# Key heads kept once and transposed in pairs, key tiles first, in a hybrid decoder block

## The reference

```python
h = rms_norm(x, norm_mix_pre)
proj = h @ w_in
u, v_sgu, q, k, v_att, gate_a, gate_b = jnp.split(proj, offs, axis=-1)
a = chunked_spatial_gating(gelu(u), gelu(v_sgu), ...)
q = partial_rotary(q.reshape(B, S, N_Q_HEADS, HEAD_DIM), positions)
k = partial_rotary(k.reshape(B, S, N_KV_HEADS, HEAD_DIM), positions)
att = sliding_window_sink_attention(q, k, v_att, sinks)   # scores of q against k in blocks of 128
merged = sigmoid(gate_a) * (a @ w_a) + sigmoid(gate_b) * (att @ w_b)
x = x + rms_norm(merged @ w_o, norm_mix_post)
hf = rms_norm(x, norm_ff_pre)
x = x + rms_norm(square(relu(hf @ w_ff_in)) @ w_ff_out, norm_ff_post)
```

## Time and profile before

| | us |
|---|---|
| median of 3 runs | 777.48 (776.97 to 778.09) |
| profiled execution, its own time | 778.64 |
| its span | 776.9 |

### The profile page before, as it was taken

The page is one execution under the profiler, slowest core; times in us unless marked ns, Lnnn a source line. Parts: engine busy times, 40 slices in busy tenths (PEclk is TensorE's granted clock), DMA queues, the critical chain, the costliest instruction groups (busy, mean ns, idle before and its releaser), DMA issues.

```text
span 776.9 us, 9953 instructions
## 1 busy us (share of the span) xinstructions
PE 764.2 (98%) x3652; PEld 642.2 (83%) x3652; DVE 528.8 (68%) x886; ACT 364.1 (47%) x607; POOL 63.6 (8%) x114
## 2 busy tenths in 40 slices
PE   7999999999999999999999999999999999999995
PEld 6888888888888888888888998888888888888885
DVE  5723577787777235875644769846885598658897
ACT  4522656665656744232225645543543345334442
POOL 2100000122223003000001200000000000000005
PEclk9999999999999999999999999999999999999998
DMA  7343132221222522326332444036102630153005
GB/s 270 117 127 108 56 106 59 79 82 55 81 77 82 196 85 78 109 82 244 90 105 76 154 145 162 28 106 248 52 1 76 240 118 1 54 204 121 0 1 109
DMA packets 92157, 81.36 MB, mean 105 GB/s; under 512 B 2896, under 2 KB 77648, under 8 KB 92112
## 3 DMA queue, kind: packets, MB, share of 16 engines
q1 hardware_dynamic: 90864, 79.70, 31.7%
q0 software_dynamic: 576, 1.05, 1.0%
q10 hardware_dynamic: 672, 0.01, 0.0%
HBM read 77.60 MB, written 3.15 MB: 104 GB/s over the span
## 4 chain that ended last, share of the span: by engine, by line
PE 92%; DVE 4%; POOL 1%; DMA 1%; issue 1%; ACT 1%; DVEq 0%; SPq 0%; POOLq 0%
PE acc L1441 27%; PE acc L1440 27%; PE acc L1439 27%; DVE w_lo L1247 1%; PE aux L1439 1%; PE aux L1441 1%; PE aux L1440 1%; DVE sum L1270 1%; PE aux L1584 1%; DMA g_pre<-in_norm_mix_pre 1%; PE aux L1583 1%; PE aux L1593 1%; PE aux L1658 1%; PE aux L1481 1%; PE acc L1612 1%
## 5 line engine op out<-in xcount | busy, mean ns | idle before, releaser
L1439 PE MATMUL acc<-actB_hi,w_hi 128*128 128x512 f32 (+1 forms) x544 | 207.0, 381 | 0.0
L1441 PE MATMUL acc<-actB_hi,w_lo 128*128 128x512 f32 (+1 forms) x544 | 205.2, 377 | 0.0
L1440 PE MATMUL acc<-actB_lo,w_hi 128*128 128x512 f32 (+1 forms) x544 | 205.0, 377 | 0.0
L965 DVE TENSOR_TENSOR w_lo<-w_raw,w_hi 128x1024 fp32r<-128x1024 f32 x72 | 87.7, 1223 | 82.7 <-ACT w_hi L682 82.1
L1441 PEld LDWEIGHTS acc<-actB_hi,w_lo 128*128 128x128 f32 x544 | 102.3, 188 | 19.0
L1440 PEld LDWEIGHTS acc<-actB_lo,w_hi 128*128 128x128 f32 x544 | 102.5, 188 | 18.2
L1439 PEld LDWEIGHTS acc<-actB_hi,w_hi 128*128 128x128 f32 x544 | 102.4, 188 | 18.1
L682 ACT ACTIVATE w_hi<-w_raw 128x1024 fp32r<-128x1024 f32 x72 | 75.4, 1052 | 71.2 <-PE acc L1441 68.8
L1440 PE MATMUL acc<-w_lo,op_hi 128*128 128x512 f32 (+1 forms) x164 | 63.6, 388 | 0.0
L1439 PE MATMUL acc<-w_hi,op_hi 128*128 128x512 f32 (+1 forms) x164 | 63.0, 384 | 0.0
L1439 PE MATMUL acc<-w_hi,actB_hi 128*128 128x512 f32 x144 | 56.1, 390 | 0.0
(11 more groups left out here) (204 smaller groups left out, 1338.9 us busy)
## 6 DMA issues: line engine op xcount, KB each, us to landing
w_raw<-in_w_in SPq DMA_DIRECT2D x44, 512.0 KB, 3.8
w_raw<-in_w_ff_in SPq DMA_DIRECT2D x32, 512.0 KB, 4.1
down_raw<-in_w_ff_out SPq DMA_DIRECT2D x16, 1024.0 KB, 6.6
w_raw<-in_w_b SPq DMA_DIRECT2D x8, 512.0 KB, 3.6
w_raw<-in_w_a SPq DMA_DIRECT2D x8, 512.0 KB, 3.5
w_raw<-in_w_o SPq DMA_DIRECT2D x8, 512.0 KB, 3.8
x<-in_x SPq DMA_DIRECT2D x4, 512.0 KB, 7.8
x<-in_x SPq DMA_DIRECT2D x1, 2048.0 KB, 8.4
```

The lines of the kernel that those rows point to most:

```text
L965: nc.vector.tensor_tensor(w_lo[:, j], w_raw[:, j], w_hi[:, j].bitcast(F32), ALU.subtract).then_inc(lo_made, 1)
L1439: nc.tensor.matmul(o, a_hi, b_hi, start=first, stop=False)
L1440: nc.tensor.matmul(o, a_hi, b_lo, start=False, stop=False)
L1441: return nc.tensor.matmul(o, a_lo, b_hi, start=False, stop=last)
```

## The change

`qk` keeps each head of k once (20 heads in place of 24), so that one transposed tile holds two different key heads and there are two k tiles in place of four. To have each head in both halves of the partitions, ScalarE writes the high part and VectorE the low part of each of the two heads into each half: four 64x512 operations on each engine for a k tile, in place of one of 128x512. The k tiles are turned first, then the q tiles; behind the four side units come 3, 3, 2 and 2 tiles. A bank and a wait now go by a tile's place in this order, not by its number. The wait for the rotated k moves ahead of the first transpose.

```diff
-NH = NQ + 2 * NKV
+NH = NQ + NKV
...
-T_FF = T_QK + KT + NKV
+QK_TILES = KT + NKV // 2
+T_FF = T_QK + QK_TILES
...
+QK_ORDER = [KT, KT + 1] + list(range(KT))
+
+
+def tiles_turned(n):
+
+    return enumerate(QK_ORDER[(0, 3, 6, 8)[n]:(3, 6, 8, 10)[n]], (0, 3, 6, 8)[n])
...
-                        nc.scalar.activation(qk[:, t, NQ:NH].rearrange("p (g r) d -> p g r d", r=2),
-                                             kv[:, 0].unsqueeze(2).to_broadcast([P, NKV, 2, HD]), ACT.Copy)
+                        nc.scalar.activation(qk[:, t, NQ:NH], kv[:, 0], ACT.Copy)
...
-                for k in range(3 * n, 3 * n + 3):
-                    act.wait_ge(turned, T_QK + k + 1)
+                for i, k in tiles_turned(n):
+                    act.wait_ge(turned, T_QK + i + 1)
...
-                            last = nc.scalar.activation(q_pair[f][0:HD, k], aux[HD * f:HD * (f + 1), k % 4], ACT.Copy)
+                            last = nc.scalar.activation(q_pair[f][0:HD, k], aux[HD * f:HD * (f + 1), i % 4], ACT.Copy)
                     else:
-                        last = nc.scalar.activation(kT_hi[:, k - KT], aux[:, k % 4], ACT.Copy)
+                        for g, half in itertools.product(range(2), range(2)):
+                            last = nc.scalar.activation(kT_hi[HD * half:HD * (half + 1), 2 * (k - KT) + g],
+                                                        aux[HD * g:HD * (g + 1), i % 4], ACT.Copy)
...
-                        last = nc.vector.tensor_tensor(kT_lo[:, k - KT], aux[:, k % 4], kT_hi[:, k - KT].bitcast(F32),
-                                                       ALU.subtract)
+                        for g, half in itertools.product(range(2), range(2)):
+                            to = (slice(HD * half, HD * (half + 1)), 2 * (k - KT) + g)
+                            last = nc.vector.tensor_tensor(kT_lo[to], aux[HD * g:HD * (g + 1), i % 4],
+                                                           kT_hi[to].bitcast(F32), ALU.subtract)
...
-                for k in range(3 * n, 3 * n + 3):
-                    if k == 0:
-                        pe.wait_ge(rotated, 1)
-                    if k == KT:
+                for i, k in tiles_turned(n):
+                    if i == 0:
                         pe.wait_ge(rotated, 2)
-                    if k >= 4:
-                        pe.wait_ge(turned_lo, T_QK + k - 3)
+                    if i >= 4:
+                        pe.wait_ge(turned_lo, T_QK + i - 3)
                     for t in range(TT):
-                        m = nc.tensor.transpose(aux[:, k % 4, t * P:(t + 1) * P],
+                        m = nc.tensor.transpose(aux[:, i % 4, t * P:(t + 1) * P],
                                                 qk[:, t, 2 * k:2 * k + 2].rearrange("p h d -> p (h d)"), ident[:])
```

More of the change, by code:

```diff
@@ L29 @@
+import itertools
 from contextlib import ExitStack
@@ L1068, in _ @@
             for n in range(SIDE_AHEAD):
-                for k in range(3 * n, 3 * n + 3):
-                    dve.wait_ge(turned_hi, T_QK + k + 1)
+                for i, k in tiles_turned(n):
+                    dve.wait_ge(turned_hi, T_QK + i + 1)
                     if k < KT:
                         for f in range(2):
-                            last = nc.vector.tensor_tensor(q_pair[f][HD:P, k], aux[HD * f:HD * (f + 1), k % 4],
+                            last = nc.vector.tensor_tensor(q_pair[f][HD:P, k], aux[HD * f:HD * (f + 1), i % 4],
                                                            q_pair[f][0:HD, k].bitcast(F32), ALU.subtract)
                     else:
-                        last = nc.vector.tensor_tensor(kT_lo[:, k - KT], aux[:, k % 4], kT_hi[:, k - KT].bitcast(F32),
-                                                       ALU.subtract)
+                        for g, half in itertools.product(range(2), range(2)):
+                            to = (slice(HD * half, HD * (half + 1)), 2 * (k - KT) + g)
+                            last = nc.vector.tensor_tensor(kT_lo[to], aux[HD * g:HD * (g + 1), i % 4],
+                                                           kT_hi[to].bitcast(F32), ALU.subtract)
                     last.then_inc(turned_lo, 1)
```

## The result

The changed kernel takes 780.36 us (median of 6 runs, 778.52 to 781.38) against 777.32 for the kernel before (6 runs, 776.88 to 778.09): ratio 1.0038, interval 1.0029 to 1.0048. It is slower by 3.0 us. The forecast, 778.9 and "the same by a hair", was 1.5 us short; the range of 777.4 to 780.8 holds the time. By the prediction's own bar, 1.55 us, this is "slower", which it had given 0.42 against 0.55 for "the same".

The account below looks back on a forecast made before the run. TensorE, busy 98% of the span, was taken to bound the kernel. Transposes -0.87, stall +2.1 and scores +0.2 sum to +1.43 us; on the median 777.48 that gives 778.9, range 777.4 to 780.8.

Parts of the forecast that it names:

- the prediction's own bar, 1.55 us: Whole kernel: a measurement can tell about 0.2%, 1.55 us, from no change; less counts as "the same".
- Transposes, -0.87: TensorE's four transpose groups: 8 of 48 transposes go, 0.109 us each, all on the path, -0.87 us.
- Covered edits at nothing: Ahead of the groups: shorter k copies, shorter k rotation and the moved wait lie under matmuls, worth nothing.
- Price of the k operations: Writing k tiles: 64x512 operations follow each other 0.60 us apart on ScalarE, 0.70 on VectorE, as for q.
- The stall, 2.1: Group 1's third tile: TensorE waits for the second k tile's low part before reusing its bank, +2.1 us.
- The scores, 0 to 0.3, taken as 0.2: First score matmul: waits for group 3's last low part, 0 to 0.3 us lost, taken as 0.2.
- Sum, +1.43: Whole kernel: fewer transposes, new stall and late scores together make it 1.43 us slower.
- The clock: Rival, behind group 1's stall: TensorE's clock falls to half, losing 1.7 us more; sum +3.1, 780.6 us; chance 0.20.
- The argument by length: Against a clock fall behind group 1's stall: its 1.9 us idle is shorter than the opening's 2.77, which brought one.
- The other argument: For a clock fall: transposes don't count as work, so none from 94.2 to 97.5; opening trace was held against it.
- The frame of the sum: Whole kernel: sum made on the profiled span, 776.9, with 1.7 us around it, carried to the median, 777.48.

Follow-up runs that it names:

- e8: The changed kernel with tile order q0, q1, k0, k1, q2 to q7 and ScalarE's last weight rounding moved behind group 3's tiles; ratio 0.9987 to the kernel before.
- e11: The kernel of e8 run once more, unchanged; ratio 0.9990 to the kernel before.
- e2: The changed kernel with two query tiles ahead of the key tiles (q0, q1, k0, k1, q2 to q7); ratio 0.9996 to the kernel before.
- e4: The changed kernel with two full-width 128x512 operations per k tile on each engine in place of four 64x512, k wrong; ratio 0.9999 to the kernel before.
- e6: One more execution of the changed kernel, unedited, with its profile; span 778.0 us.
- e7: The changed kernel with one query tile ahead of the key tiles (q0, k0, k1, q1 to q7); ratio 0.9994 to the kernel before.
- e3: The changed kernel with the two key tiles last, in group 3; ratio 1.0083 to the kernel before.
- e9: The kernel before, unchanged, run in the place of a changed kernel beside changed kernels on the same chip; ratio 0.9996.
- e1: The changed kernel run again without edit, for spans and mean clocks of more executions; ratio 1.0034 to the kernel before.

## Why the prediction was right or wrong

- **Transposes, -0.87.** Right within 0.07: e8 and e11, where nothing waits, measure -0.94 and -0.93. The -0.87 of e2 and -0.88 of e4 match to the digit by chance, as they hold the scores' wait.
- **Covered edits at nothing.** Right: no wait for the rotated k, and the first transposes came right behind side unit 0.
- **Price of the k operations.** Right: 0.60 and 0.70 apart. This is also where the rule of the Trainium skill (VectorE: DVE Perf Modes, section "Two Vector instructions with no wait between them") agrees with the trace: eight subtractions of changing halves in 5.62 us, against four full-width ones in 2.48, 0.60 apart, in e4. It is borne out but not singled out: no run has 64-partition subtractions that stay on one half.
- **The stall, 2.1.** Right: 1.92 idle, and group 1 to the next unit 3.37 us (96.27 - 92.90) against 1.23 before (the L1439 matmul at 95.38 behind the transposes at 94.15), so 2.14.
- **The scores, 0 to 0.3, taken as 0.2.** Right: 0.11 behind the first matmul and 0.06 ahead of it (it follows group 3 after 5.72 us, in e8 after 5.66).
- **Sum, +1.43.** The trace has +1.35; the terms as measured, -0.94 + 2.14 + 0.17, give 1.37. As the loss of an execution whose clock stays, the likeliest case is right.
- **The clock.** This is the step that failed, as a chance and in what a chance is of. The prediction gave 0.20 to "the clock falls" and took the case as one that holds for the kernel or does not. It holds for a share of its executions: one of four profiled, about half by the spans. A median over runs then lies between or beyond the two, and in the first measurement three of six have the long span: 781.25, 781.31 and 781.38 us against 778.52, 779.20 and 779.46. Its price, 1.7, measured 1.6.
  - The argument by length (1.9 us is less than 2.77) was too weak, since the trace of before held one fall behind one length and no length behind which the clock stayed. The later profiles have them, in the opening: ten idles of 0.83 to 2.22 us without a fall, four of 2.31 to 3.01 with one. By these a stall of 1.9 should have left the clock alone, and in e6 it did not; what else decides is not shown.
  - The other argument rests on the Trainium skill (TensorE: Matmul & The Clock Gate, on transposes). By the prediction's reading of it the clock should fall behind the stall each time. It stayed at 1.00 in three of four profiles, in the first result with nothing but transposes and the idle from 92.90 to 96.27. In e7's opening TensorE did nothing but transposes up to 12.60 us, with an idle of 2.22 among them, and the clock was 1.00 from 2 to 32 us. The prediction's own case against that statement was thinner than it reads: the earlier trace rows have the clock at 1.00 in both windows, and what rose from 7 to 11 is only the count.
- **The frame of the sum.** It was made in the span and carried to the median by one difference, as though what lies around the span were constant. It was, for before (1.7 to 1.9), and not for the changed kernel: 8 of 23 executions add 0.6 to 1.5 us. In the first result five of six did (2.4, 2.6, 2.6, 2.8, 3.3 above the span, the sixth 2.0). With 1.75 above each span that median would be 779.15, so this adds 1.2 us. No row could have shown this ahead.
- **Together.** 1.35 in every execution, 1.6 to 2 more in about half of them, and the excess: of the first result's 3.0 us some 1.8 lie in the span (median 777.4; before's, an estimate from its median time less 1.7, is 775.6) and 1.2 around it, with an open cause. That 780.36 lies in the range is in part luck: the upper end was made for a clock that falls in every execution, and the time came near it by a fall in some and an excess that the prediction did not have.

## What to carry to other kernels

When a change makes some tiles dearer to bring out of a rotating set of banks, work out when each bank comes free in the new order: the dear tiles belong where their banks are asked for late, yet well ahead of the first reader that needs them all. First was wrong here (+3.0 us), last was worse (e3, +6 us), behind two cheap tiles they cost nothing (e2: 0.6 us under before in the span, no difference clear of noise in the time). A new stall of TensorE of about 2 us should be priced as two cases, with and without a clock that falls behind it, each holding for a share of the executions. When spans and measured times disagree, as here, report both. And when two profiled executions are compared, compare the stretch that the change touches first: here the slower kernel had the shorter span.

## What the runs showed of the hardware

The same 1.9 us of idle between transposes let the granted clock go to half for 3.4 us in one profiled execution and not in three others. An idle of 0.30 us there (e7) showed no fall; one of 3.91 us ahead of the scores (e3) brought 6.8 us at half.

In the opening, where TensorE idles between 40 and 16 transposes, the fourteen profiles part by length: no fall behind 0.83, 1.10, 1.34, 1.50, 1.52, 1.65, 1.82, 1.87, 2.05 and 2.22 us, a fall behind 2.31 (e9, the kernel before), 2.73, 2.77 and 3.01 us. The two nearest, e7 and e9:

```profile
10.29 2.29 PE L1496 MATMUL aux<-ident,x 128*128 128x128 f32 x16 [2.22 <-DVE x L997]
10.03 2.98 PE L1481 MATMUL aux<-ident,x 128*128 128x128 f32 x16 [2.31 <-DVE x L984]
```

How soon the clock falls differs from one execution to the next: behind the last matmul it went to half after 2.3 us in the first result (matmul's end 769.07, fall at 771.4) and after 5.2 us in e6 (770.47, 775.7), by the window rows under e1.

The time around the span, 1.7 to 1.9 us in every execution of one program, is 2.3 to 3.3 in almost a third of those of near relatives of it; why is open.
